# Opening of a differential attention: the last rotations, the first queries and keys, and the store and load queue rearranged (decoder step, one core)

## The reference, cut to what matters

```python
q, k, v = jnp.split(xn @ w_qkv, 3, axis=-1)      # 8 heads, 2 maps of 64 each
q = rope(q, pos); k = rope(k, pos)               # x1*cos - x2*sin, x2*cos + x1*sin
# prompt: causal over its own 256 keys; sample: 256 past keys in pages, and its own 8
p = softmax(einsum('bqhmd,bkhmd->bhmqk', q, k) * 64**-0.5)
a = p[:, :, 0] - lam * p[:, :, 1]
y = rms_norm(a @ v, subln_g) * (1 - lam_init) @ w_out
```

## Time and profile before

| | |
|---|---|
| median of 3 runs | 1358.37 us (1358.01 to 1365.11) |
| the profiled execution's own time | 1361.39 us |
| its span on the trace | 1360.1 us |
| TensorE (PE) busy | 1257.7 us, 92% |
| VectorE (DVE) busy | 583.8 us, 43% |
| ScalarE (ACT) busy | 413.6 us, 30% |
| GpSimd (POOL) busy | 135.8 us, 10% |
| mean DMA rate | 250 GB/s |

### The profile page before, as it was taken

How to read it: one execution, slowest core, us unless ns; L and a number is a source line. 1 busy time by engine, 2 the same in 40 slices (tenths; PEclk the granted TensorE clock), 3 DMA queues, 4 the chain that set the end, 5 groups by cost and what they waited for, 6 DMA issues and landing times.

```text
span 1360.1 us, 21280 instructions
## 1 busy us (share of the span) xinstructions
PE 1257.7 (92%) x8660; PEld 780.7 (57%) x8660; DVE 583.8 (43%) x1162; ACT 413.6 (30%) x745; POOL 135.8 (10%) x179
## 2 busy tenths in 40 slices
PE   6599999999999899999998997998989989999997
PEld 5477678876677653333335775775667754333332
DVE  3546357566444442221225466545454362222123
ACT  3353322244344311111116332446444321111112
POOL 5100012210000101000001032000000201010000
PEclk9799998889899899999999997999999989999999
DMA  8475354354963749999993467711773837999994
GB/s 235 130 248 134 101 152 127 98 170 143 324 252 142 299 174 385 421 421 421 421 406 104 149 223 235 246 63 57 276 265 147 347 155 306 372 422 420 420 419 181
DMA packets 114076, 340.52 MB, mean 250 GB/s; under 512 B 7646, under 2 KB 75562, under 8 KB 86320
## 3 DMA queue, kind: packets, MB, share of 16 engines
q1 hardware_dynamic: 108448, 322.20, 63.1%
q0 software_dynamic: 5088, 15.73, 3.8%
q10 hardware_dynamic: 432, 1.11, 0.2%
HBM read 328.48 MB, written 10.54 MB: 249 GB/s over the span
## 4 chain that ended last, share of the span: by engine, by line
PE 80%; DMA 10%; DVE 5%; ACT 3%; issue 1%; SPq 0%; POOL 0%; ACTq 0%; DVEq 0%
PE ps L2224 14%; PE ps L571 8%; PE ps L572 8%; PE ps L573 8%; DMA arena<-in_w_exp_up 6%; PE ps L2299 6%; PE ps L2268 4%; PE ps L1449 3%; PE ps L1488 2%; PE ps L1463 2%; PE ps L1552 2%; DMA stg<-in_w_mem_k 2%; DVE wl L565 2%; PE ps L1534 1%; PE ps L829 1%; DMA stg<-in_w_mem_o 1%
## 5 line engine op out<-in xcount | busy, mean ns | idle before, releaser
L2224 PE MATMUL ps<-arena,mkv 128*64 128x512 f32 x1024 | 225.8, 593 | 9.0 <-DMA arena<-in_w_exp_up 8.1
L571 PE MATMUL ps<-bx,wh 128*128 128x320 f16 (+2 forms) x688 | 195.3, 291 | 24.4 <-DVE wl L565 14.6
L565 DVE SCALAR_TENSOR_TENSOR wl<-stg,wh 128x1024 f16<-128x1024 f32 x128 | 160.8, 1295 | 99.5 <-ACT wh L558 99.5
L572 PE MATMUL ps<-bx,wh 128*128 128x320 f16 (+2 forms) x688 | 195.5, 291 | 0.0
L573 PE MATMUL ps<-bx,wl 128*128 128x320 f16 (+2 forms) x688 | 195.2, 291 | 0.0
L558 ACT ACTIVATE wh<-stg 128x1024 f16<-128x1024 f32 x128 | 128.5, 1050 | 157.6 <-PE ps L573 129.3
L2224 PEld LDWEIGHTS ps<-arena,mkv 128*64 128x64 f32 x1024 | 75.9, 137 | 152.9 <-issue 151.1
L2439 DVE TENSOR_TENSOR arena<-ps,arena 128x512 f16<-128x512 f32 x64 | 44.1, 689 | 160.6 <-ACT arena L2385 113.6
L571 PEld LDWEIGHTS ps<-bx,wh 128*128 128x128 f16 x688 | 68.6, 100 | 48.5 <-issue 15.2
L571 PE MATMUL ps<-arena,wh 128*128 128x320 f16 x288 | 88.3, 307 | 3.7 <-DVE arena L1410 3.0
L572 PE MATMUL ps<-arena,wh 128*128 128x320 f16 x288 | 88.2, 306 | 0.0
(11 more groups left out here) (440 smaller groups left out, 1839.5 us busy)
## 6 DMA issues: line engine op xcount, KB each, us to landing
arena<-in_w_exp_gate SPq DMA_DIRECT2D x60, 1024.0 KB, 12.3
arena<-in_w_exp_up SPq DMA_DIRECT2D x60, 1024.0 KB, 14.3
arena<-in_w_exp_down SPq DMA_DIRECT2D x32, 1024.0 KB, 15.0
stg<-in_w_exp_down SPq DMA_DIRECT2D x32, 1024.0 KB, 16.4
arena<-in_cache_mem_k SPq DMA_DIRECT2D x16, 1024.0 KB, 7.3
arena<-in_cache_mem_v SPq DMA_DIRECT2D x16, 1024.0 KB, 5.1
stg<-in_w_in_a SPq DMA_DIRECT2D x28, 512.0 KB, 4.8
stg<-in_w_qkv_c SPq DMA_DIRECT2D x20, 512.0 KB, 4.3
```

Of the source, the lines that this page charges most:

```text
L565: nc.vector.scalar_tensor_tensor(wl[:, s, c], src[:, c], WSCALE, wh[:, s, c], ALU.mult, ALU.subtract).then_inc(S["w_lo"], 1)
L571: nc.tensor.matmul(out, wh[:, s, at:at + 128], hi, start=start, stop=False, **flags)
L572: nc.tensor.matmul(out, wh[:, s, at:at + 128], lo, start=False, stop=False, **flags)
L2224: last = nc.tensor.matmul(ps[64 * j:64 * j + 64, UB, :], xe[:, q % 2, j, k, :], gu[:, g % 2, j, :, k, :], start=(k == 0), stop=(k == KD - ...
```

## The change

It does the following, and no arithmetic is left out.
- **Rotation.** The rotation of unit 11 goes to banks 0 and 1 and its sines to another tile, so PE no longer waits for unit 10's. The cosines of unit 10 are made by DVE (one instruction over 640 columns) and no longer by Pool.
- **Queries and new keys.** The first prompt queries `qp` are made by DVE during unit 10. The new keys' columns of `kT` are copied by ACT during unit 9. `qd` is filled by eight copies of 64 x 128 instead of four of 64 x 256: six by ACT, two by DVE.
- **First key turn.** Its four parts go to four banks (2, 3, 6, 7), so parts 2 and 3 no longer wait for the copies of parts 0 and 1, but for `rot_done` 14 (unit 10 rotated).
- **Order in iteration 0.** The prompt unit's scores come before the batch's, on PE and in DVE's maxima.
- **Split of unit 1 of `out_c`.** ACT's half comes after its two copies of turned keys; DVE's comes in iteration 0, behind `maxima(1)` and ahead of `outputs(0)`.
- **Stores and loads.** Pool issues the two stores of values after the sixth turn, in the middle of the projection. SP issues the two stores of keys itself, after units 0 and 1 of `out_c`; then keys 2, the wait for the stores, values 1 and 2, units 2 and 3 of `out_c`, and then the turns of values and keys.

```diff
@@ -496,6 +497,19 @@
                 start = 4
+            if name == "out_c":
+                load_units(name, 0, 1)
+                sp.wait_ge(S["tr_ev"], G_Y)
+                sp.dma_start(o["p_k"][0, 0].rearrange("(t p) h m d -> p t (h m d)", p=128), ktok3[:, 0:2, :]
+                             ).then_inc(S["out_keys"], 16)
+                sp.dma_start(o["s_k"][0].rearrange("b i h m d -> (b i) (h m d)"), ktok3[0:64, 2, :]
+                             ).then_inc(S["out_keys"], 16)
+                load_keys("d", 2)
+                sp.wait_ge(S["out_keys"], 32)
+                sp.wait_ge(S["out_mem"], 96)
+                load_values("d", 1)
+                load_values("d", 2)
+                start = 1
@@ -517,12 +531,9 @@
             if name in ("memo0", "out_c", "memo1"):
-                if kind == "d":
-                    sp.wait_ge(S["out_mem"], 128)
-                    load_values(kind, 1)
-                    load_values(kind, 2)
                 for b in range(2, NB):
-                    load_keys(kind, b)
+                    if b > 2 or kind != "d":
+                        load_keys(kind, b)
@@ -1425,12 +1435,21 @@
+    def opens_with_unit(c):
+        return c["diff"]
...
+    def first_banks(c):
+        return (2, 3, 6, 7) if c["diff"] else TB + TB
...
-    def fill_view(f):
-        return ps[:, TB[f % 2], :].rearrange("p (a b) -> p a b", a=2)
+    def turn_bank(c, b, f):
+        return TB[f % 2] if b else first_banks(c)[f]
...
+    def fill_view(c, b, f):
+        return ps[:, turn_bank(c, b, f), :].rearrange("p (a b) -> p a b", a=2)
@@ -1441,12 +1460,15 @@
                 pe.wait_ge(k_in[b % 2], K_IN[kind, b])
-            if 2 * n + f // 2:
+            if b == 0 and c["diff"] and len(set(first_banks(c))) == 4:
+                if f >= 2:
+                    pe.wait_ge(S["rot_done"], 14)
+            elif 2 * n + f // 2:
...
                     at = 128 * (2 * f + i)
-                    last = nc.tensor.transpose(ps[:, TB[f % 2], 256 * i + 128 * t:256 * i + 128 * t + 128],
+                    last = nc.tensor.transpose(ps[:, turn_bank(c, b, f), 256 * i + 128 * t:256 * i + 128 * t + 128],
@@ -1508,7 +1530,7 @@
             if c["diff"]:
-                pe.wait_ge(S["qp_ready"], u + 2)
+                pe.wait_ge(S["qp_ready"], u + 2 if u else 1)
@@ -1560,14 +1582,19 @@
-        for f in range(4):
-            turn(0, f)
         if c["diff"]:
+            for f in range(4):
+                turn(0, f)
+            unit_scores(0)
             pe.wait_ge(S["qp_ready"], 2)
+            pe.wait_ge(S["qd_ready"], 1)
+        else:
+            for f in range(4):
+                turn(0, f)
...
             u, more = unit_at(c, i), i + 1 < NB
-            if u is not None:
+            if u is not None and not (i == 0 and opens_with_unit(c)):
@@ -1603,7 +1630,7 @@
             act.wait_ge(S["kt_ps"], 4 * (b0 + b) + f + 1)
-            nc.scalar.copy(kT[:, 2 * f:2 * f + 2, 0:256], fill_view(f)).then_inc(S["kt_act"], 1)
+            nc.scalar.copy(kT[:, 2 * f:2 * f + 2, 0:256], fill_view(c, b, f)).then_inc(S["kt_act"], 1)
@@ -1621,6 +1648,8 @@
         turned(0, 2)
+        if c["diff"]:
+            split_hi(act, QKV + 13, 1)
@@ -1712,13 +1751,7 @@
         def unit_queries(u):
-            t, hh = u // 2, u % 2
-            if u >= 2:
-                dve.wait_ge(S["psc_ps"], u0 + u - 1)
-            for m in range(2):
-                r = slice(64 * m, 64 * m + 64)
-                last = V.tensor_copy(qp[r, u % 2, :, 64 * m:64 * m + 64], zc[r, 4 * hh:4 * hh + 4, 64 * t:64 * t + 64])
-            last.then_inc(S["qp_ready"], 1)
+            unit_queries_dve(dve, c, u)
@@ -1743,22 +1776,15 @@
-        if c["diff"]:
-            dve.wait_ge(S["padded"], 3)
-            unit_queries(0)
-            for m in range(2):
-                for r in range(2):
-                    rows = slice(64 * m, 64 * m + 64)
-                    src = zc[rows, r:8:2, NP:T].rearrange("p j (b q) -> p j b q", b=NB)
-                    V.tensor_copy(qd[rows, r:8:2, :, 16 * r + 8 * m:16 * r + 8 * m + 8], src)
-            V.tensor_copy(kT[:, :, 256:T], zc[:, 8:16, NP:T]).then_inc(S["qp_ready"], 1)
-            split_lo(dve, QKV + 13, 1)
-        turned(0, 1)
-        turned(0, 3)
+        if True:
+            turned(0, 1)
+            turned(0, 3)
+        if opens_with_unit(c):
+            unit_maxima(0)
...
             u, more = unit_at(c, i), i + 1 < NB
-            if u is not None:
+            if u is not None and not (i == 0 and opens_with_unit(c)):
@@ -1775,6 +1801,8 @@
                 maxima(i + 1)
+            if i == 0 and c["diff"]:
+                split_lo(dve, QKV + 13, 1)
@@ -1786,8 +1814,18 @@
     TURN_BANK = (7, 4)
-    ROT_BANK = (5, 6)
+    ROT_BANK, ROT_LAST = (5, 6), (0, 1)
     rsin = xn[:, 0:2, :]
...
+    def rot_bank(i):
+        return ROT_LAST if i == 11 else ROT_BANK
...
+    def skew(i, m):
+        rows = slice(64 * m, 64 * m + 64)
+        at = KD * T + 512 * i + 8 * m
+        out = bx[rows, at:at + 544].rearrange("p (r e) -> p r e", r=2)[:, :, 0:256]
+        return (out.rearrange("p r (b w) -> p r b w", b=NB)[:, :, :, 0:8],
+                zc[rows, 2 * i:2 * i + 2, NP:T].rearrange("p r (b q) -> p r b q", b=NB))
@@ -1802,9 +1840,9 @@
                 n = 2 * (i - 4) + c
-                if n >= 2:
+                if 2 <= n < 14:
                     pe.wait_ge(S["rot_done"], n - 1)
-                nc.tensor.matmul(ps[:, ROT_BANK[c], 0:T], const("rot"), zc[:, qkv_chunk(i) + c, :], start=True,
+                nc.tensor.matmul(ps[:, rot_bank(i)[c], 0:T], const("rot"), zc[:, qkv_chunk(i) + c, :], start=True,
@@ -1841,11 +1879,23 @@
                                ).then_inc(S["tr_ev"], 1)
-            split_hi(act, QKV + i + 2, i % 2)
+            if i < 11:
+                split_hi(act, QKV + i + 2, i % 2)
+            if i == 9:
+                act.wait_ge(S["rot_done"], 8)
+                nc.scalar.copy(kT[:, :, 256:T], zc[:, 8:16, NP:T])
...
                 nc.scalar.activation(lams[:, 2:4], lams[:, 0:2], ACT.Exp).then_inc(S["gln_ready"], 1)
+        act.wait_ge(S["padded"], 3)
+        act.wait_ge(S["rot_done"], 12)
+        for i in range(3):
+            if i == 2:
+                act.wait_ge(S["rot_done"], 14)
+            for m in range(2):
+                last = nc.scalar.copy(*skew(i, m))
+        last.then_inc(S["qd_ready"], 1)
@@ -1859,7 +1909,10 @@
         nc.gpsimd.memset(zv_dead[:, 0:2048], 0.0)
-        for i in range(8, 11):
+        pool.dma_start(o["p_v"][0, 0].rearrange("(t p) h d -> p t (h d)", p=128), vtok3[:, 0:2, :]
+                       ).then_inc(S["out_mem"], 16)
+        pool.dma_start(o["s_v"][0].rearrange("b i h d -> (b i) (h d)"), vtok3[0:64, 2, :]).then_inc(S["out_mem"], 16)
+        for i in range(8, 10):
@@ -1877,14 +1930,20 @@
         def rope(i):
+            at_s = 2 * (i == 11)
...
                 dve.wait_ge(S["rot_ps"], 2 * (i - 4) + c + 1)
-                last = V.tensor_tensor(rsin[:, c, :], ps[:, ROT_BANK[c], 0:T], const("sin"), ALU.mult)
+                last = V.tensor_tensor(xn[:, at_s + c, :], ps[:, rot_bank(i)[c], 0:T], const("sin"), ALU.mult)
             link(last)
+            if i == 10:
+                at = qkv_chunk(i)
+                link(V.tensor_tensor(zc[:, at:at + 2, :], zc[:, at:at + 2, :],
+                                     const("cos").unsqueeze(1).to_broadcast([128, 2, T]), ALU.mult))
...
                 n, at = 2 * (i - 4) + c, qkv_chunk(i) + c
-                dve.wait_ge(S["rot_cos"], n + 1)
-                V.tensor_tensor(zc[:, at, :], zc[:, at, :], rsin[:, c, :], ALU.add).then_inc(S["rot_done"], 1)
+                if i != 10:
+                    dve.wait_ge(S["rot_cos"], n + 1 - (2 if i == 11 else 0))
+                V.tensor_tensor(zc[:, at, :], zc[:, at, :], xn[:, at_s + c, :], ALU.add).then_inc(S["rot_done"], 1)
@@ -1908,8 +1967,15 @@
                 rope(i - 1)
+            if i == 10:
+                dve.wait_ge(S["rot_done"], 12)
+                unit_queries_dve(dve, ATT["d"], 0)
...
         dve.wait_ge(S["rot_done"], 16)
+        dve.wait_ge(S["padded"], 3)
+        for m in range(2):
+            last = V.tensor_copy(*skew(3, m))
+        last.then_inc(S["qp_ready"], 1)
@@ -2695,13 +2761,6 @@
         qkv_pool(pool)
-        pool.wait_ge(S["tr_ev"], G_Y)
-        pool.dma_start(o["p_k"][0, 0].rearrange("(t p) h m d -> p t (h m d)", p=128), ktok3[:, 0:2, :]
-                       ).then_inc(S["out_mem"], 16)
-        pool.dma_start(o["s_k"][0].rearrange("b i h m d -> (b i) (h m d)"), ktok3[0:64, 2, :]).then_inc(S["out_mem"], 16)
-        pool.dma_start(o["p_v"][0, 0].rearrange("(t p) h d -> p t (h d)", p=128), vtok3[:, 0:2, :]
-                       ).then_inc(S["out_mem"], 16)
-        pool.dma_start(o["s_v"][0].rearrange("b i h d -> (b i) (h d)"), vtok3[0:64, 2, :]).then_inc(S["out_mem"], 16)
```

(15 more changed lines are left out.)

## The result

Nine runs of each kernel on one chip: 1361.46 us before (median, 1358.01 to 1365.11), 1352.52 after (1347.88 to 1358.08). The ratio is 0.9945, 95% interval 0.9925 to 0.9965, which is 7.5 us, between 4.8 and 10.2 (the two medians by themselves are 8.9 us apart). The profiled execution has a span of 1351.2 us (1360.1 before).

The account below looks back on a forecast made before the run. TensorE was taken to bound the kernel (80% of the chain), VectorE counting only where TensorE waits, in the attention's opening. 9.2 - 0.7 - 1.25 = 7.25 us, from 1358.37 to a median of 1351.1 us; range 1348.5 to 1356.5.

Parts of the forecast that it names:

- Steps 1 to 6: Attention's opening: shorter VectorE sequence and fewer TensorE waits bring the first mix 9.2 us sooner; bounds 6 and 10.6.
- Step 3: Opening, 824 to 827: VectorE's cosines and adds collide with GpSimd's cosines, 1.45 us of loss.
- Step 7: Iteration 1: the split ahead of outputs(0) on VectorE delays TensorE's weights by 0.7 us, between 0 and 1.15.
- Step 8: Iteration 2: keys 3, queued on SP behind out_c's last unit, which awaits the split, hold TensorE 1.25 us.
- Step 9: SP's queue: moving the stores and the wait for them is worth zero by itself.
- The rival of the half clock: Opening: idle stretches close together bring half clock back; 1353.6 to 1356.7 us, say 1355; chance 0.17.
- full clock from 822 to 920: Sign of being right: TensorE at full clock over this trace time in us; half clock within 825 to 845 meant wrong.
- the weak step: Opening: the 1.73 us wait had not lowered the clock, so full clock was assumed, with scores taking 1.28 us.
- The slower one, late key pages: Keys 3 landing 12.7 us after issue would cancel the gain; at 20 us the kernel takes 1365.7; chance 0.05.

Follow-up runs that it names:

- split_back: Changed kernel with the split on both engines where it was before, VectorE's half just ahead of the key copies; 0.9979 of the kernel before.
- two_banks: Changed kernel with the first key turn's four parts in two banks again; 0.9956 of the kernel before.
- cos_dve: Changed kernel with unit 11's cosines made by VectorE instead of GpSimd; 0.9932 of the kernel before.
- late_split: cos_dve with VectorE's split behind iteration 5 and units 2 and 3 of out_c behind all pages on SP's queue; 0.9934 of the kernel before.
- clock_fill: Changed kernel with 14 and 12 unread matmuls in TensorE's idle time in the opening; 0.9969 of the kernel before.
- keys_first: Changed kernel with values 3 and keys 3 ahead of units 2 and 3 of out_c on SP's queue; 0.9927 of the kernel before.
- split_gap: Changed kernel with VectorE's split between the prompt unit's and the batch's maxima in iteration 0; 0.9919 of the kernel before.
- queue_only: Kernel before with only the new order of SP's queue and GpSimd's early value stores; 0.9989 of the kernel before.
- the second comparison: The changed kernel run once more, no edit, against the kernel before; 0.9968, median 1353.18 against 1359.31 us.
- compute_only: Changed kernel with SP's queue and GpSimd's four stores as before; 1.005 of the kernel before.

## Why the prediction held, and where it did not

- **Steps 1 to 6, the opening: 9.2 us.** Measured 8.4 with half clock (23.3 to 15.0) and 9.5 without. Each part came out close: cosines on VectorE 0.82 (0.83 predicted), idle stretches 1.63 and 1.61 (1.7 and 1.7), `qd` copies 0.46 (0.5), key copies 1.29 (1.36), scores 8.8 after the scale (9.2). split_back and two_banks show the shares of the split and of the banks at the scores (2.3 and 2.2 us, not additive); the query and key copies and the banks of the rotation were taken out by no run alone, and their share is read from rows.
- **Step 3, the collision: 1.45 us.** The adds took 2.10 instead of 0.90, 1.2 more; shown by cos_dve.
- **Step 7, the slip of iteration 1: 0.7 us.** First to second mix 9.41 in both profiles instead of 8.94: 0.47. late_split, which has no split there, is back at 8.93.
- **Step 8, keys 3: 1.25 us.** This is the term that was mis-sized. The wait was 1.98 and 2.08. In the first profile TensorE came when forecast (8.8 us behind the end of the split), and the last page of keys 3 landed 6.1 us after its issue where I had 5.4. Half clock behind the wait about doubled the cost: from the second to the third mix 13.0 instead of 9.15, so 3.8 to 3.9 us. In cos_dve, two_banks and clock_fill the clock did not fall behind the same wait, and the cost was 2.2 to 2.7. I had put a returning clock into a rival, at the opening, and not behind the new wait. keys_first takes the whole of it away; split_gap and split_back show that the place of the split is what makes the keys late.
- **Step 9, the stores: zero.** queue_only: 0.9989, zero lies within.
- **Sum.** In the traces 8.4 - 0.5 - 3.8 = 4.1 us, and 9.5 - 0.5 - 3.9 = 5.1, where I had 7.25. The timed ratios give 7.5 (4.8 to 10.2) and, in the second comparison, 0.9968 of 1359: 4.3 (1.2 to 7.5). My 1351.1 was near the median of 1352.52, but the mechanism is worth 4 to 5 us by the traces, and the agreement of the first comparison to a quarter of a microsecond is partly luck. So is that of the time itself: I started from 1358.37, the median of three runs, and the nine of the comparison have 1361.46. Some 2 us behind the start of `out_c`, on which I had no step, may belong to the gain.
- **The rival of the half clock** (0.17) came true in the profile, for 3.4 us and 1.1 us of cost, and again behind keys 3. By my own list that is a sign of being wrong: I had asked for full clock from 822 to 920. That the idle stretches of the opening do no harm since 1.73 us before did none was the weak step; 1.63 and 1.61 us brought the clock down in one profile and not in the next. The slower one, late key pages, was the right place, but at 2.6 us over my 1.25 where 7.25 would decide. compute_only shows that it decides as soon as the queue is not rearranged.

What stays open: the size of the whole gain to better than 3 us. Neither comparison can tell 4 from 7.

## What to carry to other kernels

When work is moved off the critical sequence, look at who waits for its result: the split itself cost TensorE 0.5 us in the new place, but through the load behind it in the queue, and the pages behind that load, 2.2 to 3.9. An in-order queue makes the last wait in it everybody's wait, so loads that are needed last belong last. And a stage is best measured in the trace from one instruction to another; here the runs of the changed kernel scatter by 10 and 13 us in the two comparisons, and its stage came out the same to 1.0. Even so one trace is one throw of the clock: hold an effect of the edit apart from a fall of the clock by looking at a second profile.

## What the runs showed of the hardware

- TensorE's clock fell to half (1.2 GHz) behind two idle stretches of 1.6 us, with 2 us of work between them, in one execution and not in the next of the same kernel. The same for the idle time in iteration 2: it fell behind 1.98 and 2.08 us and stayed full behind 2.00, 2.29 and 2.5. And the same for 1.9 us in the last iteration, where the fall cost 4.3 to 4.5 us in three profiles of fourteen. That part of the scatter between runs is this fits, but no run isolates it: among the nine runs of the changed kernel the shortest (1347.88 us) has a mean clock of 0.965, the longest (1358.08) 0.958.
- From the start of the scale to the first scores all profiles with the same order agree within 0.02 us (8.79 to 8.81), so the engines' own times repeat. The differences between profiles of one kernel behind that point came with a fall of the clock.
- VectorE's add with two SBUF inputs and GpSimd's multiply hold each other up: 2.10 and 2.55 us together against 0.89 and 1.68 apart. Beside GpSimd's memset an add took its usual 0.48.
